# Expert stage of a hybrid decoder step: row lists read by another queue, four more blocks on the static path, residual rows in pieces

## What is computed

```
g_sel, e_w, expert_ids = top-1 of 8 groups, then top-2 of its 8 experts     # 64 experts, 2 per token
for each block of at most 128 rows of one expert e:
    xb = rmsnorm(h)[tokens of the block]                   # 128 x 1024
    y  = (silu(xb @ w_gate[e]) * (xb @ w_up[e])) @ w_down[e]   # 1024->256, 1024->256, 256->1024
out = h + sum over the token's two experts of gate * y
y_prompt, y_sample = rmsnorm(out) * norm_final
```

## Time and profile before

| what | value |
|---|---|
| median of 3 runs | 2615.37 us (2609.44 to 2616.18) |
| profiled execution, its own time | 2617.05 us |
| its span, first to last instruction | 2615.3 us |
| mean granted TensorE clock | 0.936 |
| PE busy over the span | 2261.3 us, 86% |
| DMA, mean over the span | 155 GB/s |
| expert blocks begin, last result landed, end | about 1750, 2531, 2615 us |

### The profile page before, as it was taken

One profiled execution on the slowest core, in us unless ns is written; L12 is line 12 of the kernel. 1 busy time (PEld: TensorE's weight loads), 2 busy tenths in 40 slices (PEclk: granted clock), 3 DMA queues, 4 the chain that ended last, 5 costly groups with the idle time before them and its releaser, 6 DMA issues. The chain is left out here.

```text
span 2615.3 us, 36391 instructions
## 1 busy us (share of the span) xinstructions
PE 2261.3 (86%) x12560; PEld 1265.2 (48%) x12560; DVE 1340.1 (51%) x2789; ACT 651.5 (25%) x1695; POOL 693.5 (27%) x909
## 2 busy tenths in 40 slices
PE   7999999999968999999999999846999999997500
PEld 3454454534546666666676667422444444443200
DVE  4415234125136554555657556354676676674328
ACT  3202122012035543444445444200000000000002
POOL 1010100100110111101130321134555555555555
PEclk9999999999978999999999999868999999999755
DMA  8041220400481121121321122165999999997437
GB/s 282 26 133 33 61 98 11 137 2 16 117 224 50 56 91 57 52 65 56 99 67 56 56 73 77 43 232 213 357 355 347 359 359 362 363 357 276 160 123 299
DMA packets 170263, 405.31 MB, mean 155 GB/s; under 512 B 49411, under 2 KB 91123, under 8 KB 145513
## 3 DMA queue, kind: packets, MB, share of 16 engines
q1 hardware_dynamic: 139351, 350.38, 37.9%
q0 software_dynamic: 24928, 35.21, 3.8%
q10 hardware_dynamic: 5842, 17.80, 1.8%
HBM read 345.12 MB, written 94.80 MB: 168 GB/s over the span
## 5 line engine op out<-in xcount | busy, mean ns | idle before, releaser
L3092 PE MATMUL p_ps<-p_w_arena,p_x_arena 128*128 128x512 f32 x1024 | 463.7, 607 | 66.1 <-DVE p_x_arena L2993 66.1
L869 PE MATMUL p_ps<-p_xt,p_w 128*128 128x512 f32 x1088 | 475.6, 595 | 0.5 <-DVE p_xt L700 0.5
L3092 PEld LDWEIGHTS p_ps<-p_w_arena,p_x_arena 128*128 128x128 f32 x1024 | 199.2, 195 | 320.7 <-issue 286.0
L869 PEld LDWEIGHTS p_ps<-p_xt,p_w 128*128 128x128 f32 x1088 | 204.7, 191 | 254.6 <-issue 249.4
L2765 POOL DMA_INDIRECT p_x_arena<-s_hn,p_slot x272 | 276.6, 1017 | 120.7 <-issue 83.9
L2427 PE MATMUL p_ps<-p_w_out,p_mixt 128*128 128x512 f32 x544 | 253.8, 611 | 0.0
L3015 DVE STREAM_TRANSPOSE p_y_arena<-p_y_arena 32x64 f32<-32x64 f32 x1024 | 240.8, 235 | 13.2
L3101 PE MATMUL p_ps<-p_w_arena,p_y_arena 128*128 128x512 f32 x512 | 231.7, 595 | 10.5 <-DVE p_y_arena L3015 10.5
L2993 DVE STREAM_TRANSPOSE p_x_arena<-p_x_arena 128x1024 f32<-128x1024 f32 x66 | 133.8, 2028 | 97.3 <-DMA p_x_arena<-s_hn,p_slot 95.6
L3101 PEld LDWEIGHTS p_ps<-p_w_arena,p_y_arena 128*128 128x128 f32 x512 | 97.7, 191 | 134.5 <-issue 134.5
L2427 PEld LDWEIGHTS p_ps<-p_w_out,p_mixt 128*128 128x128 f32 x544 | 99.9, 193 | 106.7 <-issue 104.5
(11 more groups left out here) (422 smaller groups left out, 3078.3 us busy)
## 6 DMA issues: line engine op xcount, KB each, us to landing
p_w_arena<-in_w_exp_gate SPq DMA_DIRECT2D x64, 1024.0 KB
p_w_arena<-in_w_exp_up SPq DMA_DIRECT2D x64, 1024.0 KB
p_w_arena<-in_w_exp_down SPq DMA_DIRECT2D x64, 1024.0 KB
p_w_arena<-s_y SPq DMA_DIRECT2D x16, 1024.0 KB, 13.3
p_x<-in_x_prompt SPq DMA_DIRECT2D x30, 512.0 KB, 4.7
p_w<-in_w_in SPq DMA_DIRECT2D x4, 2048.0 KB
p_spread<-s_roots SPq DMA_DIRECT2D x16, 512.0 KB, 6.8
s_kv<-p_us SPq DMA_DIRECT2D x32, 256.0 KB
```

Source lines behind the costliest of these rows:

```text
L869: ins = mm(ps[:, job % 4, :], w[:, c, at:at + P], xt[s % 2][:, c, :], start=(c == 0), stop=(c == KC - 1))
L3092: t = mm(ps[:, 2 + b, :], xt[b][:, c, :], w_gu[bw][:, :, c, :], start=(c == 0), stop=(c == KC - 1))
```

## The change

- SP reads the row lists of `gather_listed`, not POOL. There are now four buffers of raw lists. SP issues the five small DMAs of block i+4+b just ahead of the weights of block i+b, in its last loop.
- POOL's first loop runs four blocks further, so blocks 60 to 63 are gathered from the table. Its second loop starts at i = 60; there `scatter(i+b)` now stands ahead of `gather_listed(i+b+4)`.
- The residual rows are loaded in pieces: after every four blocks of weights, from block 8 on, one tile of 128 rows (0.5 MB), 13 in all. The last three tiles and the 64 sampled rows follow at the end. Ahead of the pieces SP waits for the end of the routing's list writes and for `owner_ready`.
- The table's view is declared four columns wider, so that its index may run on.

```diff
-            with sp.Fori(R, NE - R, R) as i:
+            for b in ring:
+                load_weights(R + b, R + b, b)
+            sp.wait_ge(K["ids_out"], 16 * 2 * TILES)
+            sp.wait_ge(on["owner_ready"], 1)
+            h_flat = h_all[:].rearrange("p t d -> p (t d)")
+            with sp.Fori(2 * R, NE - R, R) as i:
                 for b in ring:
                     load_weights(i + b, i + b, b)
+                sp.dma_start(h_flat[:, bass.ds(i * (D // R) + (-2 * D), D)], S["h"][bass.ds(i * (P // R) + (-2 * P), P)]
+                             ).then_inc(on["h_in"], 16)
             total = n_blocks(sp)
             with sp.Fori(NE - R, total, R) as i:
                 for b in ring:
                     e = sp.value_load(owner[0:1, bass.ds(2 * (i + (b + R - NE)), 1)], min_val=0, max_val=NE - 1)
+                    q = sp.value_load(owner[0:1, bass.ds(2 * (i + (b + 2 * R - NE)) + 1, 1)], min_val=0, max_val=NE * PLACES)
+                    sp.wait_ge(homes_own.sem, homes_own.back(i + (b + R - NE), R))
+                    with nc.allow_non_contiguous_dma(reason="one row to columns"):
+                        sp.dma_start(raw[b][:, 0:1], S["ids"][bass.ds(q, 1)].rearrange("o c -> c o")).then_inc(raw_in[b], 16)
+                        for k in range(4):
+                            sp.dma_start(raw[b][32 * k:32 * k + 32, 1:5],
+                                         S["ids"][bass.ds(q, 1)].rearrange("o (g b) -> b (o g)", g=4)).then_inc(raw_in[b], 16)
                     load_weights(i + b, e, b)
-            sp.wait_ge(K["ids_out"], 16 * 2 * TILES)
-            sp.dma_start(h_all[:, 0:NT, :], S["h"][0:SEQ].rearrange("(n p) d -> p n d", p=P)).then_inc(on["h_in"], 16)
+            early = NE // R - 3
+            sp.dma_start(h_all[:, early:NT, :], S["h"][early * P:SEQ].rearrange("(n p) d -> p n d", p=P)).then_inc(on["h_in"], 16)
...
             def gather_listed(j, b, arrived):
-                n, ts, tt = b % 2, nc.gpsimd.tensor_scalar, nc.gpsimd.tensor_tensor
-                q = pool.value_load(owner[0:1, bass.ds(2 * (j + (R - NE)) + 1, 1)], min_val=0, max_val=NE * PLACES)
+                ts, tt = nc.gpsimd.tensor_scalar, nc.gpsimd.tensor_tensor
                 pool.wait_ge(xt_ready.sem, xt_ready.back(j, R))
+                pool.wait_ge(raw_in[b], arrived)
                 apart(pool, on["slots_ready"], 1)
-                with nc.allow_non_contiguous_dma(reason="one row to columns"):
-                    pool.dma_start(raw[n][:, 0:1], S["ids"][bass.ds(q, 1)].rearrange("o c -> c o")).then_inc(raw_in[n], 16)
-                    for k in range(4):
-                        pool.dma_start(raw[n][32 * k:32 * k + 32, 1:5],
-                                       S["ids"][bass.ds(q, 1)].rearrange("o (g b) -> b (o g)", g=4)).then_inc(raw_in[n], 16)
-                pool.wait_ge(raw_in[n], arrived)
-                apart(pool, on["slots_ready"], 1)
...
-            with pool.Fori(0, NE - 2 * R, R) as i:
+            with pool.Fori(0, NE - R, R) as i:
                 for b in ring:
                     gather(i + b + R, b)
                     scatter(i + b, b % 2, 8 * i + 16 * (b // 2) + 16, 8 * i + 16 * ((b + 1) // 2) + 16)
             total = n_blocks(pool)
-            with pool.Fori(NE - 2 * R, total, R) as i:
+            with pool.Fori(NE - R, total, R) as i:
                 for b in ring:
-                    gather_listed(i + b + R, b, 40 * (i + (2 * R - NE)) + 80 * (b // 2) + 80)
                     scatter(i + b, b % 2, 8 * i + 16 * (b // 2) + 16, 8 * i + 16 * ((b + 1) // 2) + 16)
+                    gather_listed(i + b + R, b, 20 * (i + (R - NE)) + 80)
...
             evacuate_y(total - 1, 1, total * 8)
             dve.wait_ge(on["tail_in"], 32)
-            dve.wait_ge(on["h_in"], 32)
+            dve.wait_ge(on["h_in"], 16 * (NE // R - 1))
```

More of the change, by code:

```diff
@@ L2655, in moe @@
         homes = sb("homes", [P, SLOTS], I32)
-        slots = K["lg"][:].rearrange("p t n -> p (t n)")[:, 0:4 * NE].rearrange("p (g e) -> p g e", g=4)
+        slots = K["lg"][:].rearrange("p t n -> p (t n)")[:, 0:4 * (NE + R)].rearrange("p (g e) -> p g e", g=4)
         sel = cut(work, 9 * D, (4, 4, 32))
         slot = [sb(f"slot{b}", [P, 4], I32) for b in ring]
-        raw = [sb(f"raw{b}", [P, 5]) for b in two]
+        raw = [sb(f"raw{b}", [P, 5]) for b in ring]
         home_f, token_f, none_f = sb("home_f", [P, 1]), sb("token_f", [P, 4]), sb("none_f", [P, 4])
@@ L2670, in moe @@
         slot_ready = signal("slot_ready", 1, 4)
-        raw_in = [sem(f"raw{b}_in") for b in two]
+        raw_in = [sem(f"raw{b}_in") for b in ring]
         step_own, homes_own = signal("step_own", 11, 4), signal("homes_own", 1, 4)
@@ L2770, in gather_listed @@
             def gather_listed(j, b, arrived):
-                n, ts, tt = b % 2, nc.gpsimd.tensor_scalar, nc.gpsimd.tensor_tensor
-                q = pool.value_load(owner[0:1, bass.ds(2 * (j + (R - NE)) + 1, 1)], min_val=0, max_val=NE * PLACES)
+                ts, tt = nc.gpsimd.tensor_scalar, nc.gpsimd.tensor_tensor
                 pool.wait_ge(xt_ready.sem, xt_ready.back(j, R))
-                apart(pool, on["slots_ready"], 1)
-                with nc.allow_non_contiguous_dma(reason="one row to columns"):
-                    pool.dma_start(raw[n][:, 0:1], S["ids"][bass.ds(q, 1)].rearrange("o c -> c o")).then_inc(raw_in[n], 16)
-                    for k in range(4):
-                        pool.dma_start(raw[n][32 * k:32 * k + 32, 1:5],
-                                       S["ids"][bass.ds(q, 1)].rearrange("o (g b) -> b (o g)", g=4)).then_inc(raw_in[n], 16)
-                pool.wait_ge(raw_in[n], arrived)
+                pool.wait_ge(raw_in[b], arrived)
                 apart(pool, on["slots_ready"], 1)
                 def step(k):
-                    pool.wait_ge(step_own.sem, step_own.part(j + (R - NE), k))
+                    pool.wait_ge(step_own.sem, step_own.part(j + (-NE), k))
                     apart(pool, on["slots_ready"], 1)
-                quad = raw[n][:, 1:5]
-                ts(home_f[:], raw[n][:, 0:1], 0.0, None, ALU.is_equal).then_inc(step_own.sem, 1)
+                quad = raw[b][:, 1:5]
+                ts(home_f[:], raw[b][:, 0:1], 0.0, None, ALU.is_equal).then_inc(step_own.sem, 1)
                 ts(none_f[:], quad, 0.0, None, ALU.is_equal).then_inc(step_own.sem, 1)
@@ L2795, in gather_listed @@
                 step(6)
-                tt(home_f[:], home_f[:], raw[n][:, 0:1], ALU.add).then_inc(step_own.sem, 1)
+                tt(home_f[:], home_f[:], raw[b][:, 0:1], ALU.add).then_inc(step_own.sem, 1)
                 tt(token_f[:], token_f[:], quad, ALU.add).then_inc(step_own.sem, 1)
@@ L2804, in gather_listed @@
                 nc.gpsimd.tensor_copy(slot[b][:], token_f[:]).then_inc(slot_ready.sem, 1)
-                pool.wait_ge(homes_own.sem, homes_own.all(j + (R - NE)))
+                pool.wait_ge(homes_own.sem, homes_own.all(j + (-NE)))
                 fetch_rows(j, b)
@@ L2964, in _ @@
             dve.wait_ge(on["spread"], 1)
-            nc.vector.tensor_scalar(slots, ps[:, 4, 0:4 * NE].rearrange("p (g e) -> p g e", g=4), spare[:, 2:3], None, ALU.add
+            nc.vector.tensor_scalar(slots[:, :, 0:NE], ps[:, 4, 0:4 * NE].rearrange("p (g e) -> p g e", g=4), spare[:, 2:3], None, ALU.add
                                     ).then_inc(on["slots_ready"], 1)
```

## The result

The changed kernel takes 2533.8 us (median of 4 runs, 2530.5 to 2535.8) against 2613.67 us for the kernel before in the same set (4 runs, 2609.4 to 2616.2): ratio 0.9695, 95% interval 0.9677 to 0.9713, or 80 us less. I had forecast 2543 us with 2534 as the low end. The direction and the main mechanism, the listed rounds, came out; the gain was 6 to 8 us larger than forecast (6 by medians, 8 by profiles), and the median lies just outside the range.

The account below looks back on a forecast made before the run. PE was taken to set the steady pace at 10.30 us a block, and eight serial listed rounds on POOL the expert stage's end. 2617.05 - 76.4 + 3 = 2543.6, stated as 2543 us; range 2534 to 2565.

Parts of the forecast that it names:

- the listed rounds: POOL, end of expert stage: eight serial list-driven gathers of 17.08 us set the end; shortening them gives minus 76.4 us.
- scatter 55, the anchor: POOL at 2370.44 us: starting point of the sum, both kernels taken as alike up to there except for pieces of h.
- scatter 60: POOL, after four more table gathers: expected at 2416 us, the middle of bounds 2410 and 2422.
- three empty rounds: POOL, between scatters 60 and 63: gathers for nonexistent blocks, 11.66 us each without list reads, 35.0 us in all.
- scatter 63 to gain request: From POOL's last scatter to SP asking for the final gain: 3.4 us, as in the kernel before (3.37).
- cost of the pieces on PE, 1850 to 2360: Steady stretch: 13 loads of residual rows fill idle DMA time, 0.25 us each with occasional misses, 3 us in sum.
- gain request to the end of the span: Tail after SP asks for the final gain: expected unchanged, the last empty gather hidden by 4 us.
- my early end: Lower bound of about 2410 us for scatter 60 on POOL, set by when PE's result of block 60 is ready.
- The pace by the DMAs: Steady stretch: each piece costs its full 1.3 to 1.46 us, 17 to 19 us in all, total 2559; chance 0.12.
- The lists didn't clog SP's ring: Rival: list reads delay weights of blocks 60 to 63 by up to 20 us, PE waits, total 2561; chance 0.05.
- POOL's rounds did fall: Rival, end of expert stage: lists arrive late or rounds on POOL stay at 17.08 us, total 2560; chance 0.05.
- The slow rival: Steady stretch: a scatter missing its dip lands 10.3 us later, PE loses 8.9 us per piece, total 2657; chance 0.04.

Follow-up runs that it names:

- four pieces: Changed kernel with three further loads of the same rows after each piece of h: 2563.21 us, ratio 0.9828 to the kernel before.
- the three with branches in the loops: Changed kernel skipping gathers and turns beyond the last block: 2526.72 us; also with h at the end: 2527.15; or with pieces and two scatters in flight: 2524.1.

## Why the prediction was right, and where it failed

By its own steps, profiled executions against each other:

| step | forecast | measured |
|---|---|---|
| scatter 55, the anchor | 2370.4 | 2360.3 |
| scatter 60 | 2416 (2410 to 2422) | 2412.7 |
| three empty rounds | 35.0 | 35.8 |
| scatter 63 to gain request | 3.4 | 3.4 |
| cost of the pieces on PE, 1850 to 2360 | +3 | 0 (PE busy for all 510.0) |
| gain request to the end of the span | 84.5 | 82.2 |
| profiled time | 2543.6 | 2535.8 |

*The listed rounds.* Right: eight rounds in series on POOL set the end, four left it, the others lost the 5.4 us of reading. What each part is worth was not forecast, and the runs show it: moving the reads alone brought 68 us, 10.3 us a round beside the weights and h and 5.5 on quiet queues, where the prediction knew of 5.4.

*The step that failed* is "I anchor on scatter 55 at 2370.44, to where both kernels do the same but for the pieces of h", together with "so near 0, with an occasional miss: 0.25 us a piece, 3 us in sum". I had seen that scatters run one behind, and took it for a state of the loaded stretch that ends with the weights. It is a state that the kernel before is in from its first blocks, through POOL's late start, and that it did not leave in its profile, because each scatter of about 9.5 us starts only when the last has landed, 0.8 us later, which makes 10.3 again, PE's own period. So in that profile the scatters were a whole block late throughout; in the profile of the changed kernel they came back into step by about 2000 us, and scatter 60 was then bound by 2360.25 + 5 x 10.30 = 2411.8, nearer to my early end than to my middle. In the profiles the pieces brought 9 to 10 us at scatters 55 and 60 where I charged 3. The kernel with two scatters in flight shows the serial wait as the cause of the lag. What the pieces do is shown less firmly: two kernels came into step without them, so part of the 10 us is the luck of the execution. How a piece helps a scatter to catch up stays open.

*The smaller terms.* Scatter 60 came 3.3 us early, the pieces' 3 us were not paid, the third empty round took 12.94 instead of 11.66 us (one fetch idles 1.8 us there, in every kernel with the changed kernel's empty rounds and not in those where POOL reads the lists; not explained), and 2.3 us fell off behind the gain request, 2.2 of them after DVE's last instruction, in code that the change doesn't touch. One slip of the sum was too small to matter: the last rows of h are 1.8 MB, not 1.7. -3.3 - 3 + 0.8 - 2.3 = -7.8, the whole difference.

*The range* took 2370.44 as common to both sides. Its low end stood on the right early bound of scatter 60, but had no room for anything at the close; 2533.8 fell 0.2 under it. It also counted from the profiled execution, 2617.05 us, and put the 1.7 us down to the median at nothing. From the median of 2615.37 the same sum gives 2542.0 with 2532.9 as the low end, and the measured median is inside. So that it fell outside is a matter of 1 to 2 us; that the middle was 6 to 8 us off is the step above and the smaller terms.

*The rivals.* The pace by the DMAs didn't come: 371 GB/s over 510 us at PE's full pace. The Trainium skill ("DMA: Bandwidth & Descriptors", Specifications) has about 358 GB/s as the HBM limit for a core. The traces differ: 371 GB/s and, with four pieces, 386 GB/s on this one core, so the rule doesn't bind this kernel, and weighing it low was right. The lists didn't clog SP's ring (PE waited for no weights from 1825 us on), and POOL's rounds did fall, to 11.4 to 12.9 us. The slow rival (a scatter that misses its dip loses a block) has it backwards: in the profile of the kernel before the scatters had lost that block already.

## What to carry to other kernels

When a chain of transfers, each started on the landing of the last, has a period equal to the compute's, look whether it runs a whole round late: PE at 100% hides it, and it shows only where the loop ends. Where the buffers allow it, give such a chain a second transfer in flight rather than hoping for slack. And anchor a sum not on an instruction's time in the trace of before but on what sets that time; where the waits there stand at the edge, ask in which of two states it is, and put the other in the range.

## What the runs showed of the hardware

- A scatter of some 0.27 MB in 4 KB rows lands in 3.4 us on quiet queues and takes some 9.5 us beside the weights (9.4 in the median with two in flight, issue to landing); two in flight still keep up with 10.3 us a block.
- One core sustains 371 GB/s beside a fully busy PE, and 386 GB/s with PE waiting at times.
- The same 0.5 MB piece over 64 partitions in 8 KB runs costs 2 us more than over 128 partitions in 4 KB runs, with the DMA engines as busy (0.98 against 0.97) at 356 against 371 GB/s. Which of the two differences costs it isn't shown.
- Five reads of a 128-entry list as single 4-byte elements land 2.6 us after the last issue when it is quiet, 8.9 beside weights, and 6.9 beside the 8 MB of h.
- The program's close, after the last instruction of DVE, took 6.0 to 6.2, 8.3 to 8.4 or 10.3 to 10.4 us in kernels that end alike; the three with branches in the loops have the longest.
